# Projection sums made in four parts between attention units in a trunk step on one Trainium2 core

## What is computed

```python
sh1, sc1, g1, sh2, sc2, g2 = adaln(cond, w_mod, b_mod)          # six rows out of w_mod (2048 x 12288)
h = modulate(rms_norm(x, g_attn), sh1, sc1)
a_q, a_k, a_v, b_q, b_k, b_v, c_q, c_ckv, c_kr = split(h @ w_in)
o_a = attention(rope(rms_norm(a_q)), rope(rms_norm(a_k)), a_v)   # 6 heads, 2 key heads
o_b = banded_attention(b_q, b_k, b_v, sink)                      # 6 heads, 2 key heads
o_c = attention(c_q, k_c, v_c)                                   # 4 heads, keys from a compressed latent
x = x + g1 * (concat(o_a, o_b, o_c) @ w_o)
x = x + g2 * hier_moe(modulate(rms_norm(x, g_ffn), sh2, sc2))    # 32 experts, 2 per token
```

## Time and profile before

| | us |
|---|---|
| median of 3 runs | 1692.18 |
| lowest, highest | 1691.99, 1695.03 |
| span of the profiled execution | 1691.8 |
| projections beside attention | 195.49 to 489.36 |
| TensorE busy in the span | 1591.9 (94%) |
| VectorE busy in the span | 690.1 (41%) |
| ScalarE, GpSimd busy | 263.7, 106.1 |

### The profile page before, as it was taken

The page is one execution under the profiler, slowest core; times in us unless marked ns, Lnnn a source line. Parts: engine busy times, 40 slices in busy tenths (PEclk is TensorE's granted clock), DMA queues, the critical chain, the costliest instruction groups (busy, mean ns, idle before and its releaser), DMA issues.

```text
span 1691.8 us, 18209 instructions
## 1 busy us (share of the span) xinstructions
PE 1591.9 (94%) x6671; PEld 655.4 (39%) x6716; DVE 690.1 (41%) x1361; ACT 263.7 (16%) x706; POOL 106.1 (6%) x192
## 2 busy tenths in 40 slices
PE   5999999999999999999999998999999999998998
PEld 3455555544434444443332332333233233233332
DVE  3113232113245893344444345345344433544444
ACT  2004221112133000011101101110110111111010
POOL 1022100100020100000000000000000000000000
PEclk9999999999999999999999999999999999999999
DMA  9992643535199765599999999999999999999995
GB/s 394 420 385 120 230 193 119 215 109 213 54 368 410 275 264 221 203 366 426 427 429 428 428 425 428 428 424 428 427 426 428 425 424 427 428 428 423 428 427 237
DMA packets 60526, 581.94 MB, mean 344 GB/s; under 512 B 9129, under 2 KB 10121, under 8 KB 16105
## 3 DMA queue, kind: packets, MB, share of 16 engines
q1 hardware_dynamic: 53120, 557.34, 79.6%
q0 software_dynamic: 6064, 23.22, 3.6%
q10 hardware_dynamic: 1296, 0.77, 0.2%
HBM read 584.06 MB, written 7.05 MB: 349 GB/s over the span
## 4 chain that ended last, share of the span: by engine, by line
PE 68%; DMA 17%; DVE 4%; issue 2%; ACT 1%; SPq 0%; POOL 0%; ACTq 0%
PE bank L1298 24%; DMA ring<-in_w 17%; PE bank L1046 14%; PE bank L1208 7%; PE bank L1025 7%; DVE r L1794 2%; PE bank L920 2%; PE bank L1331 2%; PE bank L1133 2%; PE bank L1257 2%; PE bank L1280 1%; PE bank L1108 1%; PE bank L1194 1%; PE bank L1116 1%; PE bank L1313 1%
## 5 line engine op out<-in xcount | busy, mean ns | idle before, releaser
L1298 PE MATMUL bank<-ring,r 128*64 128x512 f32 x1920 | 469.6, 619 | 45.5 <-DMA ring<-in_w 45.5
L1298 PEld LDWEIGHTS bank<-ring,r 128*64 128x64 f32 x1920 | 129.6, 140 | 303.3 <-issue 303.3
L1046 PE MATMUL bank<-ring,r 128*128 128x384 f32 (+1 forms) x672 | 242.4, 519 | 0.0
L2014 DVE TENSOR_TENSOR bank<-bank,r 128x512 f32<-128x512 f32 x180 | 125.9, 700 | 266.2 <-PE bank L1208 266.2
L1331 PE MATMUL bank<-ring,mod_row 128*64 128x512 f32 x896 | 195.4, 593 | 7.9 <-ACT mod_row L1547 7.9
L1025 PE MATMUL bank<-ring,r 128*128 128x512 f32 x384 | 170.0, 595 | 0.0
L1046 PEld LDWEIGHTS bank<-ring,r 128*128 128x128 f32 x672 | 126.9, 191 | 103.7 <-issue 44.7
L1208 PE MATMUL bank<-r 128*128 128x512 bf16 x495 | 137.6, 382 | 7.2 <-issue 7.2
L2016 DVE TENSOR_TENSOR r<-r,bank 128x512 f32<-128x512 f32 x180 | 123.7, 687 | 6.2
L1331 PEld LDWEIGHTS bank<-ring,mod_row 128*64 128x64 f32 x896 | 75.4, 137 | 118.2 <-issue 107.9
L1208 PEld LDWEIGHTS bank<-r 128*128 128x128 bf16 x540 | 38.0, 97 | 167.4 <-DVE r L2016 97.4
(11 more groups left out here) (281 smaller groups left out, 1238.4 us busy)
## 6 DMA issues: line engine op xcount, KB each, us to landing
ring<-in_w SPq DMA_DIRECT2D x180, 2048.0 KB, 17.8
ring<-in_w_mod SPq DMA_DIRECT2D x64, 1024.0 KB, 11.8
ring<-in_w_first SPq DMA_DIRECT2D x32, 1024.0 KB, 25.9
ring<-in_w SPq DMA_DIRECT2D x19, 1024.0 KB, 9.7
ring<-in_w_o SPq DMA_DIRECT2D x16, 1024.0 KB, 6.2
r<-mod_d POOLq DMA_DIRECT2D x8, 1024.0 KB, 8.0
ring<-in_w_aq SPq DMA_DIRECT2D x8, 768.0 KB, 11.4
ring<-in_w_bq SPq DMA_DIRECT2D x8, 768.0 KB, 13.0
```

The costliest lines, as they stand in the source:

```text
L1046: mm = pe.matmul(acc[acc_of(a)][:, 0:w], h_t[:, k, t * P:(t + 1) * P], wu[:, j, :], start=(k == 0), stop=(k == KD - 1))
L1298: mm = pe.matmul(ps[64 * c:64 * c + 64, :], xg_t[:, j, 64 * c:64 * c + 64], big_cut(slot_of(u), (8, 512))[:, j % 8, :], start=(j == 0), st ...
L2014: v.tensor_tensor(ps[:, :], ps[:, :], g2b[:, min(t, 1), cols], ALU.mult).then_inc(strip_scaled, 1)
```

## The change

In the stage a projection job is made in four parts of four blocks each (a quarter of its matmuls each), and an attention unit stands behind a part:

- Group C: the 12 units lie in six jobs, (aq0, 1) to (bq0, 0), two in each: behind part 1 and behind part 3; one `mod` stands between part 2 and part 3. The tail of group C stands between the parts of (bq0, 1).
- Group A: in the six jobs of `bq1` and `bkv` the three units stand behind parts 0, 1 and 2. For (bq1, 0) they stand behind parts 1, 2 and 3. One `mod` per job is left there.
- The pending `turn` moves from behind the whole job to behind part 0, ahead of the unit there. The `norm` of such a job moves into the next job, behind its part 0 and the unit there.
- The `mod` steps that come free go, two each, behind (bq0, 2) and the three `akv` jobs. So the list has `proj` (bq0, 2), its `norm`, a `turn`, `mod` 3 15, `mod` 2 0, `proj` (akv, 0).
- The order of the ring's units follows from the list: 33 of 141 units stand at another place. No matmul, copy or transfer is added or removed.

```diff
+HOSTS_C = (("aq0", 1), ("aq0", 2), ("aq1", 0), ("aq1", 1), ("aq1", 2), ("bq0", 0))
+DRAINS_C = ("bq0", 1)
...
+    late_norm = []
+
+    def split_job(what, after):
+
+        jobs.append(what)
+        n = len(jobs) - 1
+        for i in range(4):
+            steps.append(("part", n, i) if i < 3 else ("proj", n))
+            if i == 0:
+                if len(pending) == 2:
+                    steps.append(("turn", pending.pop(0)))
+                pending.append(n)
+            for do in after[i]:
+                do()
+            if i == 0 and late_norm:
+                steps.append(("norm", late_norm.pop()))
+        assert not late_norm
+        late_norm.append(n)
...
+    def whole_job(kind, what):
+        if late_norm:
+            steps.append(("norm", late_norm.pop()))
+        job(kind, what)
...
+    c_units = [unit("C", h, t) for h in range(HEADS_C) for t in range(TILES)]
...
         for t in range(TILES):
-            attends = (name == "aq0" and t > 0) or (name == "aq1" and t < 2) or name in ("bq1", "bkv")
-            job("proj", (name, t), norm=not attends)
...
+            if (name, t) in HOSTS_C:
+                split_job((name, t), [(), (c_units.pop(0),), (fill(1),), (c_units.pop(0),)])
+            elif (name, t) == DRAINS_C:
+                split_job((name, t), [(advance,), (fill(1), advance), (fill(1), advance), (fill(1), advance)])
+                assert not c_units and not scored and not turned_p
+            elif name in ("bq1", "bkv"):
+                h0 = SHARE * (name == "bkv")
+                a, b, c = (unit("A", h0 + i, t) for i in range(SHARE))
+                if (name, t) == ("bq1", 0):
+                    split_job((name, t), [(), (turn_now, a), (b,), (c, fill(1))])
                 else:
...
+                    split_job((name, t), [(a,), (b,), (c, fill(1)), ()])
...
+                elif name in ("bq0", "akv"):
+                    mods(2)
...
+    mods(1)
+    advance()
+    steps.append(("norm", late_norm.pop()))
+    for n in (1, 1):
         mods(n)
         advance()
...
+            def in_part(n, i):
+
+                name, t = jobs[n]
+                w, at = chunk_at[name][1], acc_no[n]
+                if i == 0:
+                    acc_wait(at)
+                m = unit_no[("in", name, i)]
+                arrived(m)
+                wu = cut(ring_slot(m), (4, w))
+                for j in range(4):
+                    k = 4 * i + j
+                    mm = pe.matmul(acc[acc_of(at)][:, 0:w], h_t[:, k, t * P:(t + 1) * P], wu[:, j, :],
+                                   start=(k == 0), stop=(k == KD - 1))
```

More of the change, by code:

```diff
@@ L234, in mods, with unit, do, fill @@
         del later[:n]
+    late_norm = []
[14 more added lines that the diff above has]
+        late_norm.append(n)
+    def unit(g, h, t):
+        def do():
+            atts.append((g, h, t))
+            advance(len(atts) - 1)
+        return do
+    def fill(n):
+        return lambda: mods(n)
+    def turn_now():
+        steps.append(("turn", pending.pop(0)))
+    def whole_job(kind, what):
+        if late_norm:
+            steps.append(("norm", late_norm.pop()))
+        job(kind, what)
     for t in range(TILES):
         job("proj", ("ckv", t))
+    c_units = [unit("C", h, t) for h in range(HEADS_C) for t in range(TILES)]
     for name, _, _ in CHUNKS:
@@ L242, in plan @@
         for t in range(TILES):
-            attends = (name == "aq0" and t > 0) or (name == "aq1" and t < 2) or name in ("bq1", "bkv")
-            job("proj", (name, t), norm=not attends)
[L245 to L251, removed]
-                else:
[L253 to L256, removed]
-            else:
-                mods(2 if attends and (name, t) != ("bkv", 2) else 0)
@@ L259, in plan @@
[L259 to L270, removed]
@@ L271, in plan @@
-            if attends:
-                steps.append(("norm", n))
-    for n in (2, 1, 1):
+            if (name, t) in HOSTS_C:
[8 more added lines that the diff above has]
+                    split_job((name, t), [(), (turn_now, a), (b,), (c, fill(1))])
+                else:
+                    split_job((name, t), [(a,), (b,), (c, fill(1)), ()])
+            else:
+                whole_job("proj", (name, t))
+                if name == "cq1":
+                    if t == 0:
+                        units.append(("ukv",))
+                        steps.append(("cache", "c"))
+                        kvc(0, 0)
+                        kvc(0, 1)
+                    else:
+                        mods(3)
+                    job("proj", ("cq0", t))
+                    kvc(t + 1, 0)
+                    kvc(t + 1, 1)
+                elif name in ("bq0", "akv"):
+                    mods(2)
+                if name == "akv" and t == 0:
+                    steps.append(("cache", "a"))
@@ L1035, in _ @@
                     mod_step(s[1], s[2])
+                elif s[0] == "part":
+                    in_part(s[1], s[2])
                 elif s[0] == "proj" and s[1] not in early:
-                    name, t = jobs[s[1]]
-                    w = chunk_at[name][1]
-                    acc_wait(a)
                     for i in range(4):
[L1041 to L1051, removed]
+                        if ("part", s[1], i) not in steps:
+                            in_part(s[1], i)
                     a += 1
```

4 lines of the change are left out of this document (added).

## The result

| | before | after |
|---|---|---|
| median, us | 1692.06 (8 runs, 1691.84 to 1695.03) | 1698.18 (8 runs, 1695.91 to 1699.40) |
| span of the profiled execution | 1691.8 | 1697.2 |
| ratio of the times after / before | | 1.0033, 95% interval 1.0024 to 1.0043 |

The change makes the kernel slower by 0.33%, 6.1 us by the medians. The forecast was 1693.0, no difference to be seen, with a range up to 1697.0. The time is outside it.

What follows compares the result with a forecast made beforehand. TensorE's own list was taken to bound the stage, its gain or loss counting in full at the end. 14.0 us added against 13.15 removed gave 0.85 more: 1692.2 + 0.85 = 1693.0 us, range 1688 to 1697.

Steps and rivals of the forecast that it cites:

- What is removed: In the stage of the change: 11.4 us of TensorE waits and 1.75 of low clock, 13.15 in all, counted as removed.
- Items 1 and 2: Group C's `pt` behind `pv`: five waits, 2.95 us added; group A's `qk` behind `turn`: five waits, 3.9 us added.
- Item 3: `mod` 2 0 directly behind `mod` 3 15 waits for VectorE's addition behind the `norm` of (bq0, 2): 4.9 us added.
- Item 4: Low clock on TensorE behind the stop of 4.9 us: 1.75 us added, bounds 0 and 3.5.
- Item 5: `mod` steps standing alone in the stage, 18 instead of 6: 0.5 us added, bounds 0 and 1.5.
- What else moves, at nothing: The later `norm`, SyncE's new order of the ring's units and the release of banks and `zt` were taken to cost nothing.
- VectorE comes too late: Rival, group A: a late `norm` makes the division miss its `pt`, 1696 to 1699; chance 0.15 together with clock low twice.
- The rival without the stop: No long stop at `mod` 2 0, so items 3 and 4 fall: 1686.4; chance 0.12 together with added waits hidden.

Runs made afterwards that it cites:

- the kernel with all mends: Kernel after with the `mod` pair apart, `turn` ahead of part 0, `pv` ahead of `qk` in group C, transfers held for the `b_mod` rows: 1678.67 us.
- the one order: Kernel after with the `norm` of (bq0, 2) moved behind the two `mod` steps: 1690.88 us, ratio 0.9986 to the kernel before.
- the other: Kernel after with one `mod` behind (bq0, 2) and three behind (akv, 0): 1692.80 us, ratio 1.0000 to the kernel before.

## Why the prediction was wrong, step by step

- **What is removed**: right for the waits, wrong for the clock. The ten group A waits and the long wait at 471.94 are gone, and the kernel with all mends has a stage 11.8 us shorter, against 11.4 counted. The 1.75 of low clock at 378.32 were read from one execution and taken for a price of the waits. Three others have the same wait of 0.84 ahead of the same matmuls and take 10.55 us for them. Nothing shows that the change removed it.
- **Items 1 and 2**, five waits each at 0.59 and 0.78: right in number and place. Taken away they give 3.1 and 2.9.
- **Item 3**, the stop of 4.9: right (4.81, at 321 to 327, for the reason given).
- **Item 4**, the low clock behind it: the mechanism was right and the size wrong. 1.75 was carried over from a place with waits of 0.57 and 0.84, and behind 4.81 it measured 2.4 to 3.0 in five profiled executions, 2.9 in this one. The bound of 3.5 held it.
- **Item 5**, single `mod` steps at 0.5: not measured by itself. With items 1 to 3 as counted, the clock at 2.9 and no clock removed, the stage should have lost 0.85 + 1.75 + 1.15 = 3.75, and like for like it lost 3.3.
- **"What else moves, at nothing"** is the step that failed and took the time out of the range, with the sentence on which it rests, that the stage's gain or loss counts in full at the end. The tail keeps its length (954.09 and 954.20). The output stage doesn't: 3.3 us. The prediction looked at what SyncE's new order meant for the ring's own units (and gave `bkv` 4 to 6 places where the list has three). It didn't ask which other transfer is issued into the same stretch and is late when the ring is full. The earlier trace rows gave the share to 489.36 and from 740 us on; the stretch from 489 to 560, with a share of 1.00 to 1.02 in both kernels, was not in the argument.
- **The two measures**: the spans differ by 5.4 and the medians by 6.1. Like for like the stage gives 3.3, the output stage 3.3 and group B -0.2, which is 6.4.
- **The range**: the bounds of items 1 to 5 add up to -4.5 and +5.1 around the sum, not -3.0 and +5.3. The upper one, 1698.1, all but reaches the measured time, though by other terms, and the range stopped at 1697.

With 3.75 for the stage the sum would have been 1696.0, inside the range that was given, and with 3.3 behind it 1699.3. The rival "VectorE comes too late" gave 1696 to 1699 and so the right number by a wrong mechanism: no chain of group A came late, and its waits are gone. The rival without the stop had its price about right: 6.65 for the stop and its clock, measured 7.3 with the one order and 5.4 with the other. Its time of 1686.4 was not reached (1690.9 and 1692.8), since what `b_mod` took stays.

The Trainium skill, on the page TensorE: Matmul & The Clock Gate, section Why this matters for your kernels, asks for no long idle gap between bursts of matmuls. At 321 to 327 us the traces agree: 6.8 us at a granted clock of 0.58 follow a stop of 4.81. They also show the lower clock behind 2.70 us (578.35) and behind 0.41 and 0.70 (712 us), where the same two waits in another kernel had none, and none behind the 0.84 in three executions of four.

## What to carry to other kernels

When a stage on the bounding engine is made shorter or its transfers are moved, look at the next small transfer issued by another engine into the same full queues: here two rows arrived 2 us later and took the next engine's slack with them. Ask of every step that is put directly behind another of the same bank which instruction of the freeing engine stands ahead of the release. And test a reordering in its halves: this one held a gain of 6.6 us and a stop of 7.7 in the same stage. Before a stretch of low clock goes into a sum as something that the change removes, look at a second execution of the same code: here 1.75 us were in one of four.

## What the runs showed of the hardware

- The lower clock behind a stop costs more than one value. Behind 4.81 us it was 2.4 to 3.0 us in five profiled executions, behind 2.66 to 2.98 it was 1.4 to 2.9 in seven, behind 0.90 and 0.91 nothing (the 32 matmuls at 14.00).
- The same waits with the same instructions ahead of them are followed by the lower clock in one execution and by the full clock in another: those of 0.57 and 0.84 in one of four (1.75 us), those of 0.41 and 0.70 in six of fourteen (1.7 us in five, 3.4 in one). A row of idle time alone doesn't tell what a wait costs here.
- Two small rows fetched by GpSimd took 6.06 to 6.37 us in seven profiled executions and 4.02 to 4.06 in three, with two orders of the ring's units; the share was 1.01 during the 6.08 and 0.95 during the 4.04. With SyncE held back, VectorE's wait for them was 3.7 in four kernels, against 5.0 to 8.2 in the others. A hold of SyncE on the rows' semaphore costs nothing that could be measured (ratio 0.9999 in the kernel before). Where TensorE waited it gave 3.0 and 6.7 us by the medians, and 4.6 in both pairs of profiles up to the waits near 722 and 712.
